# Order of TensorE's work in the first attention, and of small steps at the entry of the second attention, in the FFN and at the end

## The reference, cut to what matters

```python
def gqa_block(q_blk, k, v):                 # first attention: 8 query heads, 2 key heads, head width 64
    s = einsum('bkgqd,bksd->bkgqs', q_blk, k) * (HEAD_DIM ** -0.5)
    return einsum('bkgqs,bksd->bkgqd', softmax(s), v)

ret_out = silu(rg) * head_groupnorm(ry, ret_gn_w)          # retention, one norm for each of 4 heads
q = concat([q_nope, rope(q_rope)]);  k = concat([k_nope, k_rope shared by all heads])
mla_out = causal attention of 8 heads, 96 wide keys, 64 wide values
h = h + rmsnorm((silu(hn @ w_gate) * (hn @ w_up)) @ w_down, post_ffn_norm)
h = h + rmsnorm(p @ w_ple_proj, ple_norm) * sigmoid(h @ w_ple_gate + b_ple_gate)
```

## Time and profile before

| | |
|---|---|
| median of 3 runs | 2005.74 us |
| the profiled execution | 2007.53 us |
| its span in the profile | 2005.7 us |
| mean granted TensorE clock | 0.988 |
| TensorE matmul busy | 1931.9 us, 96% of the span |
| VectorE, ScalarE, GpSimd busy | 66%, 46%, 35% |

### The profile page before, as it was taken

One profiled execution on the slowest core, in us unless ns is written; L12 is line 12 of the kernel. 1 busy time (PEld: TensorE's weight loads), 2 busy tenths in 40 slices (PEclk: granted clock), 3 DMA queues, 4 the chain that ended last, 5 costly groups with the idle time before them and its releaser, 6 DMA issues.

```text
span 2005.7 us, 25450 instructions
## 1 busy us (share of the span) xinstructions
PE 1931.9 (96%) x9539; PEld 1604.2 (80%) x9539; DVE 1314.3 (66%) x1899; ACT 917.6 (46%) x1538; POOL 694.4 (35%) x477
## 2 busy tenths in 40 slices
PE   9999999999999999987998899989999999999999
PEld 9987878887878888876777687778888888788777
DVE  5275488887785443565666557876556568968766
ACT  4121258886432222255666455633343334545551
POOL 1333325553000000006666000799999980000000
PEclk9999999999999999998999999999999999999999
DMA  5011200003224111100000334032322338886213
GB/s 201 24 40 42 74 1 1 1 1 115 85 73 148 42 32 42 34 32 22 22 22 22 136 127 158 32 116 88 112 95 84 111 111 305 276 287 213 95 32 105
DMA packets 68665, 178.49 MB, mean 89 GB/s; under 512 B 6528, under 2 KB 9856, under 8 KB 68544
## 3 DMA queue, kind: packets, MB, share of 16 engines
q1 hardware_dynamic: 44592, 121.52, 18.1%
q10 hardware_dynamic: 23952, 55.34, 7.6%
HBM read 146.95 MB, written 29.88 MB: 88 GB/s over the span
## 4 chain that ended last, share of the span: by engine, by line
PE 40%; DVE 6%; ACT 3%; issue 3%; POOL 2%; ACTq 0%; DVEq 0%; POOLq 0%
PE psc L2687 4%; PE psa L2687 4%; PE psd L2687 3%; PE psb L2687 3%; PE psa L367 3%; PE psa L2871 3%; PE psb L367 3%; PE psb L2871 3%; PE psd L367 2%; PE psc L2871 2%; PE psd L2871 2%; PE psd L2123 2%; PE psc L2090 1%; PE psc L367 1%; POOL wrf L2545 1%
## 5 line engine op out<-in xcount | busy, mean ns | idle before, releaser
L2545 POOL TENSOR_TENSOR wrf<-wr 128x512 f32<-128x512 f32 x100 | 162.1, 1621 | 119.3 <-PE psc L470 61.5
L2066 POOL TENSOR_TENSOR lps<-lps,tiny 128x128 f32<-128x128 f32 (+2 forms) x24 | 15.2, 632 | 472.9 <-DVE tiny L2061 472.8
L2558 ACT ACTIVATE wrh<-wrf 128x512 fp32r<-128x512 f32 x155 | 97.8, 631 | 157.2 <-POOL wrf L2545 82.5
L2563 POOL TENSOR_TENSOR wrl<-wrf,wrh 128x512 fp32r<-128x512 f32 x100 | 155.2, 1560 | 37.7 <-ACT wrh L2558 37.6
L399 DVE TENSOR_TENSOR wl<-wraw,wh 128x1024 fp32r<-128x1024 f32 x73 | 90.9, 1246 | 76.3 <-ACT wh L393 75.9
L367 PE MATMUL psb<-mh,wh 128*128 128x512 f32 x352 | 123.8, 396 | 2.9 <-ACT wh L393 1.6
L367 PE MATMUL psb<-ml,wh 128*128 128x512 f32 x352 | 121.6, 390 | 0.0
L367 PE MATMUL psb<-mh,wl 128*128 128x512 f32 x352 | 121.5, 389 | 0.0
L393 ACT ACTIVATE wh<-wraw 128x1024 fp32r<-128x1024 f32 x80 | 84.1, 1053 | 61.7 <-PE psb L367 28.3
L367 PE MATMUL psa<-ml,wh 128*128 128x512 f32 x288 | 103.3, 395 | 3.8 <-DVE ml L1340 2.5
L367 PE MATMUL psa<-mh,wh 128*128 128x512 f32 x288 | 104.4, 399 | 2.2 <-ACT mh L1335 1.4
(11 more groups left out here) (695 smaller groups left out, 5837.9 us busy)
## 6 DMA issues: line engine op xcount, KB each, us to landing
wraw<-slabs SPq DMA_DIRECT2D x98, 512.0 KB, 3.5
wr<-slabs SPq DMA_DIRECT2D x132, 256.0 KB, 4.1
wr<-slabs SPq DMA_DIRECT2D x40, 512.0 KB, 3.5
hidden<-hf ACTq DMA_DIRECT2D x22, 512.0 KB, 3.8
residual<-h ACTq DMA_DIRECT2D x16, 512.0 KB, 3.6
half_sums<-hsum ACTq DMA_DIRECT2D x22, 256.0 KB, 3.6
x<-xT SPq DMA_DIRECT2D x8, 520.0 KB, 8.1
h<-xT SPq DMA_DIRECT2D x8, 512.0 KB, 6.9
```

Source lines behind the costliest of these rows:

```text
L2545: e.tensor_tensor(WRF[n % NW][:, :], x, y, WEIGHTS[product(n)][2]).then_inc(*done.up(("sum", n)))
L2558: e.activation(WRH[n % NW][:, :], x, ACT.Copy).then_inc(*acted.up(("high part", n)))
L2563: e.tensor_tensor(WRL[n % NW][:, :], x, WRH[n % NW][:, :], SUB).then_inc(*pooled.up(("low", n)))
```

## The change

In the first attention the scores of unit u+1 come behind the values instead of in front of them. At the second attention's entry the two group-norm instructions of the last retention head become one function, done in step 1 behind the first query product; GpSimd makes both high rotary parts behind the norm of unit 0 and both low parts behind that of unit 1. In the retention the two norm instructions already stood next to each other, so nothing moves there. The hidden store of chunk 1 moves from w 5 to w 9. At the end the sums and the spread of the second half's norm move behind the products m 4 and m 6 (from 2 and 4), with what ScalarE and VectorE do for them; ScalarE makes the tanh of gate products 0 and 1 between the high parts of the second half, instead of behind four squares.

```diff
@@ pe_attention
                     pe_turns(e, u - LAG)
-                if u + 1 < NU:
-                    pe_scores(e, u + 1)
                 if u == NU + AHEAD - 4:
...
                 if g >= 0 and phase < 3:
                     pe_values(e, g, phase)
+                if u + 1 < NU:
+                    pe_scores(e, u + 1)
                 if u % 4 == 2 and u < NU - 4:
@@ dve_gn_gated becomes the second half of dve_gn_scaled
@@ dve_mla
-                if U == 2:
-                    dve_gn_scaled(e, RH - 1, C)
                 if w in (1, 2) and h + 1 < MH_:
                     dve_query_products(e, h + 1, w - 1)
-                if U == 6:
-                    dve_gn_gated(e, RH - 1)
+                if U == 1:
+                    dve_gn_scaled(e, RH - 1, C)
@@ pool_mla: pool_key_rotary makes r = 64 and r = 96 in one call
                 pool_mla_norms(e, U)
-                if 3 <= U < 7:
-                    pool_key_rotary(e, U >= 5, 96 if U % 2 == 0 else 64)
+                if U < 2:
+                    pool_key_rotary(e, U)
@@ act_ffn
-                if c == 2 and w == 5:
+                if c == 2 and w == 9:
                     act_hidden_store(e, 1)
@@ pe_end, and the same in act_end and dve_end
-                if m == 2:
+                if m == 4:
                     pe_f_sums(e, 1)
-                if m == 4:
+                if m == 6:
                     pe_f_spread(e, 1)
@@ act_end
-                if m == 2:
+                if m == 4:
                     act_f_root(e, 1)
...
             for m in range(KT):
                 act_h3(e, m, 1)
+                if m in (2, 5):
+                    act_ple_gate(e, m // 3)
...
+                if n >= 2:
+                    act_ple_gate(e, n)
@@ dve_end
-                if x == 2:
+                if x == 4:
                     dve_f_mean(e, 1)
-                if x == 3:
+                if x == 5:
                     dve_f_rstd(e, 1)
```

More of the change, by code:

```diff
@@ L1741, in dve_retention @@
                 dve_gn_scaled(e, h - 1, Dp)
-                dve_gn_gated(e, h - 1)
             if h in (1, 2):
@@ L1814, in dve_gn_scaled @@
                                    op0=MUL, op1=MUL).then_inc(*vec.up(("gn scaled", n)))
-        def dve_gn_gated(e, n):
             e.wait_ge(*vec.on(("gn scaled", n)))
@@ L2245, in dve_mla, with pool_key_rotary @@
                     dve_split_half(e, MX, 0, "mix2", EARLY[b - NM2 + 4:b - NM2 + 5])
-        def pool_key_rotary(e, low, r):
+        def pool_key_rotary(e, low):
             key = KRR[64:96, :]
             e.wait_ge(*vec.on(("kr", 1)))
[L2251 to L2257, removed]
+            for r in (64, 96):
+                e.wait_ge(*pooled.now())
+                if low:
+                    e.tensor_tensor(QKS[1][3][r:r + 32, :], key, QKS[1][2][64:96, :], SUB
+                                    ).then_inc(*pooled.up(("kr low", 1, r)))
+                else:
+                    e.tensor_tensor(QKS[1][2][r:r + 32, :], key, ONE[64:96, 0:1].to_broadcast([32, T]), MUL
+                                    ).then_inc(*pooled.up(("kr high", 1, r)))
             e.wait_ge(*pooled.now())
@@ L3208, in act_end, with act_ple_gate @@
                     act_e_square(e, {1: 4, 2: 5, 4: 6, 5: 7}[n])
[L3209 to L3215, removed]
+                if n >= 2:
+                    act_ple_gate(e, n)
+        def act_ple_gate(e, n):
+            m, h = 4 * (n // 8) + 2 * (n // 4 % 2) + n % 2, n // 2 % 2
+            e.wait_ge(*psum.on(("ple gate", m, h)))
+            if n == 0:
+                e.wait_ge(*vec.on("b half"))
+            if m >= 4:
+                e.wait_ge(*vec.on(("out", "all", m - 4, h)))
+            e.activation(half(OB[m % 4], h), PS[GATE_PAIR[m % 3]][:, h, :], ACT.Tanh, scale=0.5, bias=TINY[:, 40 + m:41 + m]
+                         ).then_inc(*acted.up(("ple gate", m, h)))
         def act_e_square(e, m):
```

## The result

The changed kernel takes 2010.96 us (median of 20 runs, 2006.54 to 2016.61), the kernel before 2008.20 in the runs beside it (20 runs, 2003.48 to 2012.34). The ratio is 1.0019, 95% interval 1.0011 to 1.0027: **3.8 us slower** (2.2 to 5.4). The forecast was 0.9 us faster. The time lies inside the forecast's range of 1997.5 to 2012, the sign is the other one.

The account below looks back on a forecast made before the run. TensorE was taken to bound the steady first attention (busy 49.99 of 50 us). Attention +13.1, entry -10.6, FFN 0, end 0 and -3.4 sum to -0.9: 2004.8 us, own range from bounds 1999.5 to 2010, 8-in-10 range 1997.5 to 2012.

Parts of the forecast that it names:

- The term for the wait behind ScalarE's copy: First attention, phase 0: value matmul waits for ScalarE's copy, 1.01 us in each of thirteen groups, +13.1 us.
- The upper bound for the attention: First attention: 1.3 us a group (+17) if the late maximum also holds the transposes of phase 0.
- (a): Second attention's entry: low parts no longer wait behind the norm's second half; TensorE's 3.11 us becomes 0.7, -2.4 us.
- (b): Second attention's entry: TensorE's 6.57 us wait for head 1's rotary key goes, -6.6 us.
- (d): Second attention's entry: both norm instructions on VectorE between the query products delay the chain; +1.0 us, worst +2.5, best -0.5.
- one engine holding the other for a whole instruction: Entry, reading of GpSimd and VectorE contention: would make (d) +2.2 us and the whole sum 1.2 us longer.
- (e): End: TensorE's 2.03 us for the sums isn't won, product m 3 waits for m 0's copy; 0, bounds -1 and +1.
- (f): End, before gate product n 5: wait of 3.08 becomes 1.3 us (-1.8), half-clock window behind it goes (-1.6).
- Rival 1: First attention: new wait only 0.5 us as ScalarE's copy moves forward; attention costs 6.5, time 1998.2 us; chance 0.17.
- Rival 2: Entry: GpSimd's queue becomes the wait, entry gains 4.5, time 2010.9 us; chance 0.17 (with Rival 4).
- Rival 3: First attention: clock falls in half of the 13 groups, costing 10.4 us, time 2015.2; chance 0.09.
- Rival 4: Entry: another wait for head 1, such as its low key, replaces the rotary key's; 2011.4 us; chance counted with Rival 2.

Follow-up runs that it names:

- experiment 5: Kernel before with the attention's new order alone, and GpSimd's staging of the next queries' high part one step later (phase 3); +13.9 us against before.
- experiment 7: Kernel before with the attention's new order alone, ScalarE's copies in front of phase 3's exponential and GpSimd's staging one step later; +0.4 us against before.
- experiment 1: Kernel before with only the new order of scores and values in the first attention; +17.7 us against before.
- experiment 2: Changed kernel with the old order in the first attention, so only the entry, the store and the end changed; -11.6 us against before.
- experiment 12: Kernel before with only GpSimd's rotary parts in their new places, the norm's halves staying in steps 2 and 6; -4.8 us against before.
- experiment 13: Kernel before with only the changes of the end and the hidden store; -6.8 us against before.
- experiment 11: Kernel before with only both halves of the norm in step 1 behind the first query product; -2.6 us against before.
- experiment 8: experiment 2's kernel with GpSimd's low rotary parts behind the norm of unit 2 instead of unit 1; -15.5 us against before.

## Why the prediction was wrong, point by point

**The step that failed** is, as the prediction put it, "In the other phases I find no new wait: the bank of the exponentials and the low parts are in time with some 0.5 us or more". They aren't. With the scores at the end of a step, VectorE's maximum starts at the head of the next one and stands in front of the low parts. What the other phases cost is:
- In phase 2 of every second group VectorE's small norm slides into GpSimd's staging, ends only with it and holds the low parts, and these hold the transposes. Phase 2 is 0.32 us longer by it and the phase 3 behind it 0.16: 2.6 us over the attention, which experiment 5 takes away. This is the new wait that the step denied.
- Phase 2 of every group is 0.10 longer, 1.3 us in all. No row shows a wait there, and its cause is open.
- In phase 3 the maximum starts at T+0.20, and the low parts behind it release the next transposes at T+2.41 instead of T+2.21. Beside the wait for ScalarE's copy this costs nothing, and with the copies moved 0.02 us (6.17 against 6.15 for phases 3 and 0 in experiment 7).

The term for the wait behind ScalarE's copy was right: 0.96 us a group in phases 3 and 0 against 1.01, without the staging. So the attention's +13.1 should have been about +17 (17.0 in the trace, 17.7 in experiment 1). With it the forecast would have been +3.0 us instead of -0.9; +3.8 was measured.

The upper bound for the attention, +17, has the right number by luck. It came from 1.3 us a group "if the maximum, which now always starts a step late, also holds the transposes of phase 0". The maximum does hold them, by 0.20, but phases 3 and 0 cost 0.96 us all the same; the 4 us came from phase 2, which that bound doesn't name. The "own range, from the bounds" of 1999.5 to 2010 isn't their sum either: the bounds as written add up to a change of -11 to +12 us.

**Entry.** -10.6 was forecast, the trace has -11.0, with (a) at 2.5, (b) at 6.6 and the clock of the head behind at 1.00. By the spread of the traces with the old entry the gain is anything from 8.9 to 12.1, so that the closeness is partly chance. And VectorE's part of the price (d) was mis-sized. I took L1949 from 1.40 to 1.92 by the nearest row; the new neighbour made it 3.44 in the changed kernel, 4.45 in experiment 2 and 5.21 in experiment 12. Against the trace of before the unit 4 scores came 1.2 us later in the changed kernel (near my +1.0) and 3.6 in experiment 2 (beyond my +2.5). But the clock's stretches are in these numbers. Against experiment 7, whose old entry has full clock up to there, the changed kernel's come 1.7 later; against experiment 13, with the stretch in the same place, experiment 2's come 2.5 later, at my worst bound. The Trainium skill, GPSIMD Engine Reference, section "Key points", says that the two engines contend on SBUF interfaces when VectorE has two SBUF inputs, and I had worked out the reading "one engine holding the other for a whole instruction" and set it aside. The traces agree with that reading (4.45 us for the low key beside 5.12 of GpSimd). It would have made the forecast +0.3 us instead of -0.9. The terms (a) and (b) also weren't independent, as the trace of experiment 11 shows: the gain of (a) alone goes into (b)'s wait. In the sum of both this doesn't show.

**FFN and end.** Term 0 for the sums holds. The store's move won 0.5 us of the wait of 4.04, inside its bounds of -1 and +1, though the prediction expected nothing from it. TensorE's 2.03 us for the sums became 2.03 for the copy of m 0, as written in (e). Term (f) is right in the trace, wait and clock: -3.4.

**Rivals.** Rival 1 fell: no copy came earlier by itself. Rival 2 did not happen as priced: GpSimd's norms of units 2 and 3 released no wait in the changed kernel; but its idea, rotary parts in the wrong place of a queue, is what experiment 2 shows through VectorE. Rival 3 fell: TensorE stands still for 0.71 us a group and more, and the clock stays at 1.00. Rival 4 fell: the scores of unit 8 (936.16) start without a wait. None of them had the slower result for its reason.

## What to carry to other kernels

When work is moved inside a step of a pipeline, follow the engine that consumes it through every phase of the period, and ask which of its small instructions slides into a long one of a neighbour; a bound that says so deserves a look at the timelines and not a guess. A row that shows an instruction slowed by 0.5 us beside another engine says nothing of the slowdown beside a longer one. And where a new order exposes a wait, the cure may be as small as the cause: two instructions of ScalarE in front of one, and one of GpSimd a step later, took a cost of 17 us back to about 1 in the trace (+0.4 us in the median, not told from none).

## What the runs showed of the hardware

A VectorE instruction with two SBUF inputs that starts while a GpSimd instruction runs does not run slower in proportion; by these traces it waits for that instruction's end. L1224 (4 elements a partition) took 0.16 to 0.27 us alone and 1.33 beside a GpSimd instruction of 1.89, and both ended within 0.02 us of each other. The low key, 1.40 us for two instructions alone, took 4.45 beside two of GpSimd of 5.12 in all: it began 1.22 us after the first of them and ended 0.55 us after the last (907.53 and 906.98), about the 0.7 that its own second instruction needs. GpSimd loses some time too: its pair of L2249 is 5.12 to 5.48 us long, against twice 2.35 and a gap of 0.17 as between such a pair in experiment 12. VectorE's instructions with an input in PSUM kept their times beside the same neighbours (L1955 at 917.15 in the changed kernel's timeline, beside GpSimd's high parts, took 0.69 us, as in the earlier trace rows). The six stagings of the changed kernel show the same: L1224 takes 1.24 to 1.34 us beside each and 0.16 in the groups between. This is read from timelines. Experiments 5 and 8 changed only which instructions meet, and the durations followed (1.33 to 0.16, 4.45 to 1.92).

The place where the TensorE clock falls at a chain of waits is not the same in two traces of the same code. In before it was 0.53 from 889.80 to 893.30 and full in the next query product; in experiments 2 and 13 it was full there and fell at that next product (rows of 0.57 to 0.72 us where full clock has 0.39 to 0.50).
